# Two gate chunks of the even layer's modulation summed by VectorE, the other four chunks' halves placed in a row

## What is computed

```python
def adaln(cond, w_mod, b_mod):
    m = jax.nn.silu(cond) @ w_mod + b_mod
    return _split(m, (D_MODEL, D_MODEL, D_MODEL))
...
        sh_l, sc_l, ga_l = adaln(c, w_mod[layer], b_mod[layer])
        sh_c, sc_c, ga_c = adaln(c_ctx, w_mod[layer], b_mod[layer])
        h_lat = rms_norm(x_lat, g_pre[layer]) * (1 + sc_l[:, None]) + sh_l[:, None]
        h_ctx = rms_norm(x_ctx, g_pre[layer]) * (1 + sc_c) + sh_c
...
        x_lat = x_lat + ga_l[:, None] * rms_norm(y_lat, g_post[layer])
```

## Time and profile before

| | us |
|---|---|
| median of 3 runs (lowest, highest) | 1784.21 (1783.65, 1784.56) |
| span of the profiled execution | 1780.9 |
| TensorE busy | 1732.2 (97%) |
| VectorE busy | 1164.9 (65%) |
| ScalarE busy | 914.3 (51%) |
| loads of weights: halves of 1 MB, median to landing, in the even projection | 5.1 |

### The profile page before, as it was taken

The page is one execution under the profiler, slowest core; times in us unless marked ns, Lnnn a source line. Parts: engine busy times, 40 slices in busy tenths (PEclk is TensorE's granted clock), DMA queues, the critical chain, the costliest instruction groups (busy, mean ns, idle before and its releaser), DMA issues. The chain is left out here.

```text
span 1780.9 us, 22805 instructions
## 1 busy us (share of the span) xinstructions
PE 1732.2 (97%) x8527; PEld 1394.0 (78%) x8527; DVE 1164.9 (65%) x2141; ACT 914.3 (51%) x1490; POOL 49.4 (3%) x68
## 2 busy tenths in 40 slices
PE   8999999999998999999999999999999999999998
PEld 3776788777787877777777787788887787878886
DVE  6653466698437557767866775777646867577744
ACT  4333444333336356655656556467534756547743
POOL 0000000000000000000100002000000002000000
PEclk9999999999999999999999999999999999999999
DMA  9466211121425444443544444555554454555562
GB/s 333 155 200 226 95 56 64 54 70 67 142 95 175 132 125 146 147 139 107 180 147 153 147 154 155 176 177 193 198 189 157 127 175 134 183 165 183 189 218 76
DMA packets 115972, 267.23 MB, mean 150 GB/s; under 512 B 5412, under 2 KB 9837, under 8 KB 115672
## 3 DMA queue, kind: packets, MB, share of 16 engines
q1 hardware_dynamic: 111384, 252.26, 43.3%
q0 software_dynamic: 3504, 10.96, 2.0%
q10 hardware_dynamic: 976, 2.57, 0.4%
HBM read 264.63 MB, written 1.14 MB: 149 GB/s over the span
## 5 line engine op out<-in xcount | busy, mean ns | idle before, releaser
L146 DVE TENSOR_TENSOR qw_rest<-weights,qw_lead 128x1024 fp32r<-128x1024 f32 (+2 forms) x428 | 520.1, 1222 | 380.5 <-ACT qw_lead L334 375.3
L334 ACT ACTIVATE qw_lead<-weights 128x1024 fp32r<-128x1024 f32 (+2 forms) x428 | 446.4, 1048 | 461.5 <-PE psum L173 421.6
L173 PE MATMUL psum<-qw_lead,b_h_pair 128*128 128x512 f32 (+1 forms) x960 | 319.9, 398 | 3.3 <-ACT b_gates L2927 1.4
L173 PEld LDWEIGHTS psum<-qw_lead,b_h_pair 128*128 128x128 f32 x960 | 180.4, 188 | 43.8 <-issue 3.7
L173 PE MATMUL psum<-qw_rest,b_h_pair 128*128 128x512 f32 (+1 forms) x480 | 186.2, 388 | 0.0
L166 PE MATMUL psum<-b_h_pair,qw_lead 128*128 128x512 f32 x512 | 178.1, 392 | 2.0 <-DVE b_h_pair L713 2.0
L167 PE MATMUL psum<-b_h_pair,qw_rest 128*128 128x256 f32 x512 | 143.3, 280 | 0.0
L173 PE MATMUL psum<-e_h_lead,qw_lead 128*128 128x512 f32 x320 | 141.0, 441 | 1.8 <-DVE e_qT L1532 1.4
L173 PE MATMUL psum<-e_h_lead,qw_rest 128*128 128x512 f32 x320 | 125.7, 393 | 0.0
L173 PE MATMUL psum<-e_h_rest,qw_lead 128*128 128x512 f32 x320 | 124.9, 390 | 0.0
L166 PEld LDWEIGHTS psum<-b_h_pair,qw_lead 128*128 128x128 f32 x512 | 95.8, 187 | 23.7 <-DVE b_h_pair L713 2.9
(11 more groups left out here) (481 smaller groups left out, 3011.9 us busy)
## 6 DMA issues: line engine op xcount, KB each, us to landing
weights<-in_w_in SPq DMA_DIRECT2D x48, 1024.0 KB, 5.1
weights<-in_o_w_in SPq DMA_DIRECT2D x32, 1024.0 KB, 5.4
weights<-in_w_mlp_up SPq DMA_DIRECT2D x32, 1024.0 KB, 5.5
weights<-in_w_mlp_down SPq DMA_DIRECT2D x32, 1024.0 KB, 4.9
weights<-in_e_w_in SPq DMA_DIRECT2D x26, 1024.0 KB, 5.1
weights<-in_w_mod SPq DMA_DIRECT2D x24, 1024.0 KB, 7.1
weights<-in_e_w_out SPq DMA_DIRECT2D x8, 1024.0 KB, 4.9
weights<-in_o_w_out SPq DMA_DIRECT2D x8, 1024.0 KB, 4.9
```

What stands on the lines that cost most here:

```text
L146: return eng.tensor_tensor(self.rest[at], src, self.lead[at].bitcast(F32), ALU.subtract)
L173: mm = nc.tensor.matmul(out, l, r, start=start and i == 0, stop=stop and i == 2)
L334: self.core.nc.scalar.activation(self.buf.lead[self.at(u)], self.raw(u), ACT.Copy).then_inc(self.lead_ready, 1)
```

## The change

The stream's order is changed. `cols` takes the quarters (counted over the projection) before which a modulation half goes: one beside kv's last quarter, three beside q's quarters 0, 2 and 3, two beside q2's last two, six beside gatt's first six. Halves are then, from half 8 on: kv, kv, M0, q, M1, q, M2, M3, q2, q2, M4, M5, gatt, M6, M7, gatt, M8, M9, gatt, M10, M11, gatt. `slots` gives their units: 3, 4, 6, 7, then 10 to 17.

M0 to M3 are chunks (0, 4) and (0, 5). A new stage, `SideMods`, sums them without TensorE: for each half, each of its four blocks and each condition one instruction of 128x512, the block times its condition value (one number per partition) added to one of two accumulators. `by_vector=(0, 1)` puts both conditions on VectorE. Their nominal times are twice the slot plus 0.45 for each block and 0.2 for the context. TensorE turns both accumulators, eight transposes into two banks, at nominal 11.3 and 17.3. The ring place of such a half is free when its products are done (`wait_used`). M4 to M11 are handled as before, by a second `Mods` stage at nominal 19.9 to 33.9. The stage's `Feed` no longer has `late`.

```diff
+MODS1 = ((0, 4), (0, 5), (1, 0), (1, 1), (1, 2), (1, 3))
...
-    def cols(name, w, starts, width=BANK, chunks=None):
+    def cols(name, w, starts, width=BANK, beside=()):
         first[name] = len(units)
-        for s in starts:
+        for i, s in enumerate(starts):
             for r in range(w.shape[0] // BANK):
                 at = len(halves)
                 halves.append([(w[r * BANK:(r + 1) * BANK, s:s + width].rearrange("(k p) n -> p k n", p=P), 0, 4, width)])
-                chunk = chunks.pop(0) if chunks else None
                 for q in range(2):
-                    if chunk:
-                        mod_half(*chunk, q)
+                    if 4 * i + 2 * r + q in beside:
+                        first["mod1"].append(len(units))
+                        mod_half(*chunks.pop(0))
                     units.append((at, q * 2 * width, 2, width, True))
...
     mods("mod0", 0, (0, 2, 1, 3))
     w = a["e_w_in"][0]
-    cols("e_kv", w, (EV_KV,))
-    chunks = [(0, 4), (0, 5), (1, 0), (1, 1), (1, 2), (1, 3)]
-    cols("e_q", w, (EV_Q,))
-    cols("e_q2", w, (EV_Q + 512,), chunks=chunks)
-    cols("e_gatt", w, (EV_GATT, EV_GATT + 512), chunks=chunks)
+    chunks = [(l, j, r) for l, j in MODS1 for r in range(2)]
+    first["mod1"] = []
+    cols("e_kv", w, (EV_KV,), beside=(3,))
+    cols("e_q", w, (EV_Q,), beside=(0, 2, 3))
+    cols("e_q2", w, (EV_Q + 512,), beside=(2, 3))
+    cols("e_gatt", w, (EV_GATT, EV_GATT + 512), beside=range(6))
...
+    def quarters(self, name, n):
+
+        u = self.first[name]
+        return [v for v in self.split_units if v >= u][:n]
...
         for m in self.raws:
-            for u, at in zip(m.units, m.at):
-                free.append((w.units[u][0], at, w.chunk, w.done_at(u)))
+            for n, (u, at) in enumerate(zip(m.units, m.at)):
+                free.append((w.units[u][0], at, m, n))
         for h, at, sem, value in sorted(free, key=lambda z: z[0]):
             yield at + self.offsets[2]
             if h + w.RAW < len(w.halves):
-                sp.wait_ge(sem, value)
+                if isinstance(sem, Mods):
+                    sem.wait_used(sp, value)
+                else:
+                    sp.wait_ge(sem, value)
                 w.load(sp, h + w.RAW)
...
+    def wait_used(self, sp, n):
+        sp.wait_ge(self.core.stream.chunk, self.core.stream.done_at(self.units[n]))
+
+    def parts(self):
+        return self.core.ps[:, self.spread_bank[0], :].rearrange("p (b c r) -> p b r c", b=4, c=4)[:, :, 0:2, :]
...
+class SideMods(Mods):
...
+    def __init__(self, core, tag, room, chunks, units, at, accs, banks, ready, free, turn_at, by_vector=(0,)):
+        super().__init__(core, tag, room, chunks, units, at, (), (), (banks[1],), None, free, turn_at=turn_at, take_at=[z + 0.3 for z in turn_at])
+        for u in units:
+            core.stream.uses(u, 0)
+        self.accs, self.pair, self.begin = accs, banks, ready
+        self.added = [core.sem(tag + name) for name in ("added_main", "added_ctx")]
+        self.tensor, self.scalar = (self.turns,), ()
+        self.vector = tuple((self.main_adds, self.ctx_adds)[s] for s in by_vector) + (self.takes,)
+        self.gpsimd = tuple((self.main_adds, self.ctx_adds)[s] for s in range(2) if s not in by_vector)
+
+    def wait_used(self, sp, n):
+        for sem in self.added:
+            sp.wait_ge(sem, 4 * n + 4)
...
+    def adds(self, eng, s):
+        w, cond, added = self.core.stream, self.room.cond, self.added[s]
+        for n, u in enumerate(self.units):
+            i, r = n // 2, n % 2
+            acc = self.accs[i % 2][s]
+            for c in range(4):
+                yield self.at[n] + 0.45 * c + 0.2 * s
+                if c == 0:
+                    self.begin(eng, n)
+                    w.wait_landed(eng, w.units[u][0])
+                    if r == 0 and i >= 2:
+                        eng.wait_ge(self.spread, self.spread_at(i - 2))
+                z, weight = w.raw(u).rearrange("p (k n) -> p k n", k=4)[:, c, :], cond[:, 4 * r + c, s:s + 1]
+                if r + c == 0:
+                    ins = eng.tensor_scalar(acc, z, weight, None, ALU.mult)
+                else:
+                    eng.wait_ge(added, 4 * n + c)
+                    ins = eng.scalar_tensor_tensor(out=acc, in0=z, scalar=weight, in1=acc, op0=ALU.mult, op1=ALU.add)
+                ins.then_inc(added, 1)
+
+    def turns(self, pe):
+        nc, ps, bank = self.core.nc, self.core.ps, self.spread_bank[0]
+        for i, (l, j) in enumerate(self.chunks):
+            yield self.turn_at[i]
+            if i == 0:
+                self.free(pe)
+            if i:
+                pe.wait_ge(self.summed, self.summed_at(i - 1) + 2 * (i - 1 == self.gate_i))
+            for s in range(2):
+                pe.wait_ge(self.added[s], 8 * i + 8)
+                for b in range(4):
+                    mm = nc.tensor.transpose(ps[:, self.pair[s], b * P:(b + 1) * P], self.accs[i % 2][s][:, b * P:(b + 1) * P], self.core.ident[:])
+            mm.then_inc(self.spread, 1)
+            if i == self.gate_i:
+                yield self.rows_at()
...
-    u = first["e_kv"]
-    items = [Item(**span(range(u, u + 4), 0.0, 2.0), groups=tokens(BANK), src=r.h, act=kv_act, dve=kv_dve, ready_k=enter.wait_ready)]
-    u = first["e_q"]
-    items.append(Item(**span(range(u, u + 4), 8.0, 2.0), groups=tokens(BANK), src=r.h, **heads_out(0)))
-    u = first["e_q2"]
-    items.append(Item(**span(range(u + 1, u + 8, 2), 16.0, 2.0), groups=tokens(BANK), src=r.h, **heads_out(BANK)))
-    u = first["e_gatt"]
-    silu = lambda k: lambda act, src: nc.scalar.activation(core.hT[:, k, :], src, ACT.Silu)
+    items = [Item(**span(stream.quarters("e_kv", 4), 0.0, 2.0), groups=tokens(BANK), src=r.h, act=kv_act, dve=kv_dve, ready_k=enter.wait_ready)]
+    items.append(Item(**span(stream.quarters("e_q", 4), 8.0, 2.0), groups=tokens(BANK), src=r.h, **heads_out(0)))
+    items.append(Item(**span(stream.quarters("e_q2", 4), 16.0, 2.0), groups=tokens(BANK), src=r.h, **heads_out(BANK)))
+
+    def silu(k):
+        def out(act, src):
+            if k == 6:
+                act.wait_ge(mods1.spread, mods1.spread_at(0))
...
-    raws = [first["e_q2"] + 2 * n for n in range(4)] + [first["e_gatt"] + 2 * n for n in range(8)]
...
-    mods1 = Mods(core, "m1_", r, [(0, 4), (0, 5), (1, 0), (1, 1), (1, 2), (1, 3)], raws, [15.9 + 2 * n for n in range(12)],
-                 (r.rows2,), (4,), (5,), second_free, lambda pe: None)
+    def accs_free(eng, n):
+        if n == 0:
+            enter.wait_rows(eng)
+            eng.wait_ge(filt.absd, 8)
+            eng.wait_ge(filt.F_done, 8)
+        elif n == 2:
+            eng.wait_ge(enter.turned, KC)
+    slots = (3, 4, 6, 7, 10, 11, 12, 13, 14, 15, 16, 17)
+    early, late = first["mod1"][:4], first["mod1"][4:]
+    mods1 = SideMods(core, "m1_", r, MODS1[:2], early, [2.0 * n for n in slots[:4]],
+                     ((core.hT[:, 6, :], core.hT[:, 7, :]), (r.rows2, core.ga[:, 2, BANK:2 * BANK])), (4, 5), accs_free, second_free,
+                     [2.0 * slots[2 * i + 1] + 3.3 for i in range(2)], by_vector=(0, 1))
+    mods1b = Mods(core, "m1b_", r, MODS1[2:], late, [2.0 * n - 0.1 for n in slots[4:]], (r.rows2,), (4,), (5,),
+                  lambda pe: pe.wait_ge(mods1.summed, mods1.gate_i + 3), lambda pe: None)
...
-    feed = Feed(core, (dense,), (mods0, mods1), prime=(-4.4, -4.3, -2.0), late=(first["e_q2"], 1.75), defer=True)
-    run_stages(core, [dense, enter, filt, mods0, mods1, rotary, head_turn, feed, gate_consts, Program(gpsimd=(fetch_gates,))])
+    feed = Feed(core, (dense,), (mods0, mods1, mods1b), prime=(-4.4, -4.3, -2.0), defer=True)
+    run_stages(core, [dense, enter, filt, mods0, mods1, mods1b, rotary, head_turn, feed, gate_consts, Program(gpsimd=(fetch_gates,))])
```

More of the change, by code:

```diff
@@ L1123, in takes @@
             dve.wait_ge(self.spread, self.spread_at(i))
-            parts = ps[:, self.spread_bank[0], :].rearrange("p (b c r) -> p b r c", b=4, c=4)[:, :, 0:2, :]
             sums = self.columns[:, 8 * j:8 * j + 8] if j < 4 else core.gate[:, 24 + 8 * j:32 + 8 * j]
-            nc.vector.tensor_reduce(sums.rearrange("p (b s) -> p b s", s=2), parts, AX.X, ALU.add).then_inc(self.summed, 1)
+            nc.vector.tensor_reduce(sums.rearrange("p (b s) -> p b s", s=2), self.parts(), AX.X, ALU.add).then_inc(self.summed, 1)
             if i == self.gate_i:
@@ L1152, in gate_columns, with main_adds, ctx_adds, parts @@
             core.dve_chain(dve, ins) if s < 1 - l else ins.then_inc(self.summed, 1)
+class SideMods(Mods):
[11 more added lines that the diff above has]
+            sp.wait_ge(sem, 4 * n + 4)
+    def main_adds(self, eng):
+        yield from self.adds(eng, 0)
+    def ctx_adds(self, eng):
+        yield from self.adds(eng, 1)
+    def adds(self, eng, s):
[32 more added lines that the diff above has]
+                yield self.rows_at()
+                pe.wait_ge(self.summed, i + 2)
```

(18 more changed lines are left out.)

## The result

The changed kernel takes 1816.5 us, median of 4 runs (1815.7 to 1818.7), the kernel before 1784.4 beside it (1783.7 to 1785.6): a ratio of 1.018, 95% interval 1.0167 to 1.0194. The forecast was 1815.9. The profiled span went from 1780.9 to 1813.9, 33.0 us more.

What follows compares the result with a forecast made beforehand. TensorE, busy 97% of the span, was taken as the bound. -3.9 (removal) + 16.9 (backlog) + 12.0 (copies) + 0.3 (head's turn) + 6.4 (clock) = +31.7 us, giving a median of 1815.9; 8-in-10 range 1796 to 1821.

Steps and rivals of the forecast that it cites:

- TensorE's queue is the bound: Stage the change touches: TensorE almost never stops, so time taken off comes off the end and waits add to it.
- What is taken off: TensorE: four of twelve modulation halves go, -4.8 us; eight transposes per turn instead of four, +0.9; net -3.9 us.
- VectorE's backlog: Up to the gate take (nominal 18.0): VectorE's 20.4 us of products and its idle waits make TensorE wait 16.9 us.
- The copies: Turns of chunks 2 to 4: ScalarE's copies stand behind splits awaiting loads; TensorE waits 4.1, 3.7, 4.1 us, +12.0.
- the head's turn: Behind the third copy wait, after a table load and the first gate outputs: a head's turn waits some 0.3 us more.
- The clock: Half clock after three 4 us waits and the one at nominal 18.0, 1.6 us each: +6.4, bounds 0 and 8.
- time around: Whole kernel: the median of the runs lies 3.3 us above the profiled span, counted as time around it.
- C: Rival: loads come before the copies are due, only VectorE's backlog counts; +14.6, 1799 us; chance 0.12.
- B: Rival: VectorE's backlog is absorbed, only the three copies wait; +12.9, 1797 us; chance 0.13.
- D: Rival: the lead of the queues hides every wait, only the removal is left; -3.9, 1780.3 us; chance 0.06.
- E: Rival: waits cancel against the gain, within 0.2%; needs all waits under 7.5 us; chance 0.04.
- F: Rival: more waits than counted, from gate broadcasts amid weight loads or a turn slipping into attention; +8, 1824; chance 0.07.

Runs made afterwards that it cites:

- b_narrow: Kernel before, with matmuls of the four modulation halves in the first query block 64 columns wide instead of 512: 1779.7 us, ratio 0.997.
- a_spread: Changed kernel with `late` back, products spread, ScalarE copying the whole first query block, filter combinations and rotation later: 1782.3 us against 1784.8, ratio 0.9988.
- a_noctx: Changed kernel with 14 of VectorE's 32 products left out (context sums keep only their first block): 1808.6 us, ratio 1.0134 to the kernel before.
- a_act: Changed kernel with `late` put back and all four groups of the first query block copied by ScalarE: 1799.3 us, ratio 1.0078 to the kernel before.
- a_late: Changed kernel with `late` (splits 1.75 later from the first query2 unit on) put back: 1798.3 us, ratio 1.0071 to the kernel before.
- b_nolate: Kernel before with only `late` taken out of its feed: 1807.7 us, ratio 1.0126.
- a_fill: Changed kernel with 15 unused 128x128 matmuls ahead of each of the three turns that wait for ScalarE's copies: 1811.4 us, ratio 1.0149.
- a_early: Changed kernel with `late` back and the first two halves' products moved from nominal 6.0 and 8.0 to 4.4 and 6.4: 1792.6 us, ratio 1.0042.

## Why the prediction was right

**TensorE's queue is the bound.** Shown by b_narrow: 3.0 us off it, from the four halves beside q2, are 3.0 off the stage.

**What is taken off, forecast -3.9.** The stage has eight groups of eight modulation records (L1080) from 132.05 to 201.35, 64 as foretold. The gain is about -3.5 in a_spread. The eight transposes cost what was counted: there the first turn takes 0.79 from start to start, 83.53 to 84.32, against 0.89 in the earlier trace rows. The rest of the 0.4 was not traced to a line.

**VectorE's backlog, forecast 16.9 with the gate's take at 123.0.** The waits up to there sum to 0.67 + 0.43 + 0.47 + 7.65 + 6.33 = 15.55 us, and TensorE is there at 124.06. The 2.0 us that half clock costs behind the query2 bank delay nothing more, as TensorE would else wait for VectorE; the prediction counts them into this term, which then is 17.55. The count holds to within half a microsecond as far as the split at 93.42 (forecast 93.7, idle 4.9, seen 5.12; load issued at 87.4, seen at 87.01). Behind it two takes were mis-sized: the sum over a full accumulator (L1143, 128x1024) takes 1.22 us each, where the whole of the gate takes had been put at 1.2 together; the second with its four small steps alone runs from 121.99 to 124.0. That is some 2 us more; in all, the way behind the split took 30.6 us against 29.3 forecast. The places were named rightly but for one, the sizes were not: the first turn was forecast at about 3.5 us and the bank at 6; seen were 0.9 and 7.65, and 0.67 at a kv bank that the prediction didn't name. a_noctx and a_act show why this didn't matter: the sum is set by VectorE's way to the gate's take, and a wait removed ahead of it comes back at the next place. Only its pieces move.

**The copies, forecast 12.0.** Seen 3.74 + 3.55 + 3.86 = 11.15, by the mechanism told: a_late takes them away, b_nolate brings them about in the old kernel. The 0.3 for the head's turn did not show.

**The clock, forecast 6.4, bounds 0 and 8.** Of the 10.1 us lost, 2.0 lie ahead of the gate's take. The prediction held that such a stretch is taken from the wait behind it, and a_noctx and a_act bear that out. This leaves 8.1 against 6.4, at the edge of the bounds. Each copy wait cost 1.7 (a_fill), against 1.6. The miss is behind the gate's take: there the clock fell while TensorE was still waiting and stayed low for 5.9 us of work, which cost 3.0, where 1.6 had been counted.

**The sum.** -3.3 + 17.55 + 11.15 + 8.1 = +33.5 us in the stage, of which 0.4 is won ahead of it (kv starts at 51.10 instead of 51.53), 33.0 in the span; here -3.3 is what is left when the rest is taken from the measured lengths, 168.66 (51.10 to 219.76) - 135.19 = 33.47. By kind, the copies with their clock cost 16.3 (forecast 16.8), the backlog with its clock 20.6 (forecast 18.5), the removal brings 3.3 to 3.5 (forecast 3.9). The median rose by 32.1 and the span by 33.0, as the median lies 2.6 us above the profiled span of after and lay 3.3 above that of before. So 1815.9 against 1816.5 owes something to that last difference; by the mechanisms alone the forecast was 1.3 us low. Nor was the 3.3 all "time around" the span, as the prediction has it: wherever one execution has both figures they are 1.8 apart, which puts the profiled execution of before at 1782.7, quicker than all that were timed with it. By term the forecast was 0.6 low on the removal, 0.65 low on the backlog, 1.15 high on the copies and 1.7 low on the clock. The mechanism was right; that the terms' errors partly cancel, and the median's distance with them, is luck of a microsecond or so.

**The rivals.** C (only the backlog) is what a_late shows: 1799 in the count, 1798.3 measured. B (only the copies) has no run of its own; b_nolate, the nearest, has five waits in place of three. D, that everything is hidden, forecast 1780.3, is a_spread in the main: its room on VectorE exists, as the prediction said, but not in the order in which the change puts the work. E would have needed two of the three kinds of wait to be absent, and all three are there. F, more waits, did not show: from the first matmul behind the stage to the end it is 1594.1 us after and 1594.2 before.

## What to carry to other kernels

Before work is moved to an engine with idle time, write down what stands behind it in that engine's order and when each of these is wanted: 20 us of products fitted into VectorE's idle time, but of the orders tried only in the one with their nominal times spread and other work moved behind the take. Next, look at what a deferral protects before it is dropped; here a split that waits for a load stood ahead of a copy that was ready, which cost some 16 of the 32 us. And count TensorE's waits together with the half clock behind them (here 1.7 us for each of the three waits of 3.55 to 3.86, and 3.0 behind the gate's take), but not where another wait for the same late engine follows: there only that engine's way counts.

## What the runs showed of the hardware

- Four matmuls with 32 output rows each, 512 columns wide, cost TensorE no more than one: 0.99 us for the eight records of a half, 0.97 for two. To take such work off, its columns have to go, not its matmuls.
- What the clock costs behind a wait is no constant. After the 7.65 us it was 4.0 us of work at half clock, after the 6.33 it was 5.9; in a_act 6.4 after a wait of 5.59 and 5.8 after one of 3.90. Nor is it sure that it falls: it did not after waits of 2.48 (a_noctx) and 3.59 us (b_nolate, at 171.15), and did after one of 1.79 (a_early). So a kernel can lose through this what it gained elsewhere, as a_act did behind the gate's take.
- A sum of VectorE's over 128x1024 from PSUM takes 1.22 us, like a two-tensor instruction of that size.
